# Gather of the token rows one pair ahead, kept totals inside the last gate-up product, last down weights in column halves, and the down biases in the third expert pair

## What is computed

```python
def expert_step(acc, xs):
    wgu, bgu, wdn, bdn, c = xs
    gu = jnp.matmul(hx, wgu) + bgu
    gate = jnp.minimum(gu[:, 0::2], SWIGLU_LIMIT)
    up = jnp.clip(gu[:, 1::2], -SWIGLU_LIMIT, SWIGLU_LIMIT)
    act = gate * jax.nn.sigmoid(SWIGLU_ALPHA * gate) * (up + 1.0)
    y = jnp.matmul(act, wdn) + bdn
    return acc + c[:, None] * y.astype(jnp.float32), None
...
hx = layer_norm(DN_ALPHA * hx + f, ln2_g, ln2_b)
```

## Time and profile before

| what | before |
|---|---|
| time, median of 3 runs (lowest to highest) | 1141.97 us (1140.39 to 1142.9) |
| time of the profiled execution | 1139.37 us |
| its span, first to last instruction | 1137.5 us |
| TensorE matmul busy | 1099.5 us (97%) |
| VectorE busy | 293.1 us (26%) |
| ScalarE busy | 203.6 us (18%) |
| mean DMA rate over the span | 399 GB/s |

### The profile page before, as it was taken

The page is one execution under the profiler, slowest core; times in us unless marked ns, Lnnn a source line. Parts: engine busy times, 40 slices in busy tenths (PEclk is TensorE's granted clock), DMA queues, the critical chain, the costliest instruction groups (busy, mean ns, idle before and its releaser), DMA issues.

```text
span 1137.5 us, 14116 instructions
## 1 busy us (share of the span) xinstructions
PE 1099.5 (97%) x5468; PEld 463.2 (41%) x5469; DVE 293.1 (26%) x734; ACT 203.6 (18%) x481; POOL 30.0 (3%) x65
## 2 busy tenths in 40 slices
PE   8999999999999999999999999999999999999996
PEld 6876764433333333333333333333333333333331
DVE  1553757530303030212121212120203031303033
ACT  2323412411111120202020202020201111111102
POOL 0110111000000000000000000000000000000001
PEclk9999999999999999999999999999999999999998
DMA  9967878999999999999999999999999999999994
GB/s 361 351 219 248 285 280 336 426 433 407 430 421 430 430 431 430 431 430 429 432 431 432 432 430 432 432 432 429 433 430 432 432 430 432 431 430 430 425 426 160
DMA packets 59172, 454.37 MB, mean 399 GB/s; under 512 B 6467, under 2 KB 19411, under 8 KB 31348
## 3 DMA queue, kind: packets, MB, share of 16 engines
q1 hardware_dynamic: 56642, 440.97, 92.7%
q0 software_dynamic: 1728, 10.75, 2.5%
q10 hardware_dynamic: 754, 1.98, 0.4%
HBM read 450.14 MB, written 11.93 MB: 406 GB/s over the span
## 4 chain that ended last, share of the span: by engine, by line
PE 83%; DMA 13%; ACT 2%; DVE 2%; issue 1%; SPq 0%; DVEq 0%
PE bank L1171 30%; PE bank L1224 19%; DMA ring<-in_w_gate_up 13%; PE bank L732 6%; PE bank L759 6%; PE bank L1055 5%; PE bank L1251 3%; PE bank L762 2%; PE bank L920 2%; PE bank L1051 1%; PE bank L1354 1%; PE bank L1267 1%; PE bank L877 1%; ACT ybuf L1417 1%; ACT actT L1417 1%; PE bank L851 1%
## 5 line engine op out<-in xcount | busy, mean ns | idle before, releaser
L1171 PE MATMUL bank<-ring,xg 128*64 128x512 f32 x2032 | 445.6, 594 | 10.8 <-DMA ring<-in_w_gate_up 10.8
L1171 PEld LDWEIGHTS bank<-ring,xg 128*64 128x64 f32 x2032 | 146.4, 137 | 299.3 <-issue 296.9
L1224 PE MATMUL bank<-ring,actT 128*64 128x512 f32 x960 | 216.2, 597 | 4.2 <-ACT actT L1417 4.2
L2080 DVE TENSOR_TENSOR acc<-acc,bank 128x512 f32<-128x512 f32 x60 | 41.3, 688 | 492.0 <-PE bank L1251 491.8
L1571 ACT ACTIVATE sig<-gate 128x256 f32<-128x256 f32 x64 | 26.5, 416 | 530.1 <-DVE gate L2062 530.1
L1224 PEld LDWEIGHTS bank<-ring,actT 128*64 128x64 f32 x960 | 67.3, 137 | 120.0 <-issue 115.3
L2062 DVE TENSOR_SCALAR gate<-bank 128x256 f32<-128x256 f32 x64 | 26.8, 419 | 186.8 <-PE bank L1171 186.8
L759 PE MATMUL bank<-xT,wblk 128*128 128x288 f32 x256 | 65.4, 409 | 0.3 <-DVE xT L1670 0.3
L1562 ACT ACTIVATE xg<-bank,small 128x128 f32<-128x128 f32 x128 | 48.0, 457 | 97.0 <-PE bank L732 96.9
L1055 PE MATMUL bank<-hx,pick 128*128 128x512 f32 x128 | 59.2, 605 | 0.0
L1417 ACT ACTIVATE ybuf<-bank 128x512 f32<-128x512 f32 x63 | 36.0, 596 | 126.7 <-PE bank L1224 87.4
(11 more groups left out here) (247 smaller groups left out, 672.3 us busy)
## 6 DMA issues: line engine op xcount, KB each, us to landing
ring<-in_w_gate_up SPq DMA_DIRECT2D x127, 2048.0 KB, 26.5
ring<-in_w_down SPq DMA_DIRECT2D x63, 2048.0 KB, 28.0
wblk<-in_w_in SPq DMA_DIRECT2D x11, 1024.0 KB, 8.7
kring<-in_cache_k_moba SPq DMA_DIRECT2D x16, 256.0 KB, 7.5
vring<-in_cache_v_moba SPq DMA_DIRECT2D x16, 256.0 KB, 7.2
out<-in_state_k_win POOLq DMA_DIRECT2D x8, 512.0 KB, 5.2
out<-in_state_v_win POOLq DMA_DIRECT2D x8, 512.0 KB, 6.1
kring<-in_state_k_win SPq DMA_DIRECT2D x16, 256.0 KB, 5.3
```

Of the source, the lines that this page charges most:

```text
L1171: ins = nc.tensor.matmul(bank[n][64 * e:64 * e + 64, :], xg[:, k, 64 * e:64 * e + 64], w[e][:, 512 * n:512 * n + 512], start=False, stop=( ...
L1224: ins = nc.tensor.matmul(bank[4 + half][64 * e:64 * e + 64, :], actT[:, j, 64 * e:64 * e + 64], w[e][:, at:at + 512], start=(j == 0), stop ...
L2080: V.tensor_tensor(o, o, new, ALU.add).then_inc(S.added, 1)
```

## The change

It does five things. `gather(i + 2)` stands behind k = 5 of `gate_up(i + 1)`, and only `gather(1)` still stands behind `gate_up(0)`; ACT takes the gathered rows at the end of `between_pairs`. In the last pair `combine` moves to k = 1, the first three `keep_sums` into `gate_up` behind k = 4 (`keep_first`, in banks 4, 5 and 7), and both activation halves are turned in bank 6. The last row chunk of `w_down` is loaded in two column halves, and ACT copies both halves of the last result, the lower one when its own matmuls are done. The products of the down biases go from pair 12 to pair 2. Some loads share a semaphore: the attention table now counts on `blk_in` and `ln_g` on `bdn_in`, and DVE waits for the second LayerNorm's parameters later.

```diff
+    Y_BANK, SUM_BANK = (0, 1), ((4, 5), (2, 3), (7,))
...
-    MIDDLE = 12
+    MIDDLE = 2
...
-            for c in range(2):
-                sp.dma_start(dst[:, :, c, :], src[:, :, 2 + c, :]).then_inc(half_in[8 + c], 16)
+            sp.dma_start(dst[:, :, 0, :], src[:, :, 2, :]).then_inc(half_in[8], 16)
+            for half in range(2):
+                h = slice(512 * half, 512 * half + 512)
+                sp.dma_start(dst[:, :, 1, h], src[:, :, 3, h]).then_inc((S.lower_in, half_in[9])[half], 16)
...
         def finish(i, m, odd, m_next, whole=True, next_whole=True):

-            gather(i + 1, i * 2)
+            if isinstance(i, int) and i == 0:
+                gather(1, 0)
             turn_weights(i, i * 2 + 3)
             turn_act(i, i * 2 + 4)
             down(i, m, odd, {0: lambda: turn_slots(i + 1, 0),
                              1: lambda: (pe.wait_ge(S.actT_ready, i * 2 + 2), turn_slots(i + 1, 1))}, whole)
             if m_next is not None:
-                gate_up(i + 1, m_next, (odd + 1) % PERIOD, {3: lambda: combine(i)}, next_whole)
+                gate_up(i + 1, m_next, (odd + 1) % PERIOD, {3: lambda: combine(i), 5: lambda: gather(i + 2, i * 2 + 2)}, next_whole)
...
-            gather(i + 1, i * 2)
             turn_weights(i, i * 2 + 3)
             turn_act(i, i * 2 + 4)
             down(i, m, odd, {0: first_slots, 1: other_slots, 2: other_biases}, True)
             pe.wait_ge(S.bias_added, 5)
-            gate_up(i + 1, m_next, (odd + 1) % PERIOD, {3: lambda: combine(i)}, True)
+            gate_up(i + 1, m_next, (odd + 1) % PERIOD, {3: lambda: combine(i), 5: lambda: gather(i + 2, i * 2 + 2)}, True)
...
-        finish(2, 0, 2, 1)
+        finish_with_biases(MIDDLE, 0, 2, 1)

         def finish_three(m):
             finish(m * PERIOD, m, 0, m)
             finish(m * PERIOD + 1, m, 1, m)
             finish(m * PERIOD + 2, m, 2, m + 1)

-        with pe.Fori(1, MIDDLE // PERIOD) as m:
+        with pe.Fori(1, PAIRS // PERIOD - 1) as m:
             finish_three(m)
-        finish_with_biases(MIDDLE, MIDDLE // PERIOD, 0, MIDDLE // PERIOD)
-        finish(MIDDLE + 1, MIDDLE // PERIOD, 1, MIDDLE // PERIOD)
-        last = PAIRS - 1
-        finish(last - 1, last // PERIOD - 1, 2, None)
+        last, final = PAIRS - 1, PAIRS // PERIOD - 1
+        finish(last - 3, final, 0, final)
+        finish(last - 2, final, 1, final)
+        finish(last - 1, final, 2, None)

         def keep_sums(t, half, stop=False):

             if t == 2:
-                return nc.tensor.matmul(bank[7][:, 0:256], ident, acc_s[:, :], start=True, stop=stop)
-            return nc.tensor.matmul(bank[2 * t + half][:, :], ident, acc[:, t, 512 * half:512 * half + 512],
+                return nc.tensor.matmul(bank[SUM_BANK[2][0]][:, 0:256], ident, acc_s[:, :], start=True, stop=stop)
+            return nc.tensor.matmul(bank[SUM_BANK[t][half]][:, :], ident, acc[:, t, 512 * half:512 * half + 512],
                                     start=True, stop=stop)

-        def last_down():
-
-            turn_act(last, 2 * last + 2, (0,))
+        def keep_first():
             pe.wait_ge(S.added, 5 * last + 5)
             keep_sums(0, 0)
             keep_sums(0, 1)
-            pe.wait_ge(S.actT_ready, last * 2 + 1)
             keep_sums(2, 0)
+
+        def turn_last(a):
+            pe.wait_ge(S.act_ready, last * 4 + 2 * a + 2)
+            pe.wait_ge(*((S.actT_ready, 2 * last + 1) if a else (S.spread_ready, last + 1)))
+            for j in range(4 * a, 4 * a + 4):
+                f = 512 * a
+                ins = turn(bank[6][:, 128 * (j % 4):128 * (j % 4) + 128], up[:, f + j % 4:f + 512:4])
+            ins.then_inc(S.act_turned, 1)
+
+        def last_down():
+
+            turn_last(0)
             for v in range(4):
                 w = ring[slot_of(0, 8 + v)]
                 if v < 3:
...
                 pe.wait_ge(S.actT_ready, last * 2 + (1 if v < 2 else 2))
                 for c in range(2):
                     j = 2 * v + c
-                    if v == 3:
-                        pe.wait_ge(half_in[8 + c], 16)
+                    if j == 6:
+                        pe.wait_ge(half_in[8], 16)
                     for half in range(2):
+                        if j == 7:
+                            pe.wait_ge((S.lower_in, half_in[9])[half], 16)
                         for e in range(2):
                             at = 2048 * e + 1024 * c + 512 * half
-                            ins = nc.tensor.matmul(bank[4 + half][64 * e:64 * e + 64, :], actT[:, j, 64 * e:64 * e + 64],
+                            ins = nc.tensor.matmul(bank[Y_BANK[half]][64 * e:64 * e + 64, :], actT[:, j, 64 * e:64 * e + 64],
                                                    w[:, at:at + 512], start=(j == 0), stop=(j == KC - 1))
+                        if j == 7 and half == 0:
+                            ins.then_inc(S.lower_done, 1)
                 if v < 3:
                     ins.then_inc(S.unit_used, 1)
                 if v == 0:
-                    turn_act(last, 2 * last + 2, (1,))
+                    turn_last(1)
                     keep_sums(1, 0)
                 if v == 1:
                     keep_sums(1, 1)

         def mix_last():

-            pe.wait_ge(S.y_ready, last * 2 + 2)
             for j in (0, 1, 4, 2, 3):
                 t, half = divmod(j, 2)
+                pe.wait_ge(S.y_ready, last * 2 + (1 if j == 0 else 2))
                 if t == 2:
-                    ins = mix_samples(bank[7], False)
+                    ins = mix_samples(bank[SUM_BANK[2][0]], False)
                 else:
-                    ins = nc.tensor.matmul(bank[j][:, :], spread[:, 128 * t:128 * t + 128],
+                    ins = nc.tensor.matmul(bank[SUM_BANK[t][half]][:, :], spread[:, 128 * t:128 * t + 128],
                                            ybuf[:, 512 * half:512 * half + 512], start=False, stop=True)
                 ins.then_inc(S.mixed, 1)

-        gate_up(last, last // PERIOD, 0, {3: lambda: combine(last - 1), 5: lambda: turn_weights(last, 2 * last + 1)})
+        gate_up(last, last // PERIOD, 0, {1: lambda: combine(last - 1), 4: keep_first, 5: lambda: turn_weights(last, 2 * last + 1)})
...
-        def take_turned(i, halves=(0, 1)):
+        def take_turned(i, halves=(0, 1), banks=(7, 6)):
             for a in halves:
                 act.wait_ge(S.act_turned, i * 2 + (a + 1))
-                copy(actT[:, 4 * a:4 * a + 4, :], bank[7 - a][:, :].rearrange("p (k s) -> p k s", k=4)).then_inc(
+                copy(actT[:, 4 * a:4 * a + 4, :], bank[banks[a]][:, :].rearrange("p (k s) -> p k s", k=4)).then_inc(
...
         sigmoids(0)
-
-        def between_pairs(i):
-            take_gathered(i + 1)
+        take_gathered(1)
+
+        def between_pairs(i, gathers=True):
             take_weights(i)
             take_turned(i)
             take_slots(i + 1)
             take_down(i)
+            if gathers:
+                take_gathered(i + 2)

         def between_with_biases(i):
-            take_gathered(i + 1)
...
-        between_pairs(PAIRS - 2)
+        between_pairs(PAIRS - 2, False)
         sigmoids(PAIRS - 1, (0, 1))
         take_weights(PAIRS - 1)
-        take_turned(PAIRS - 1, (0,))
+        take_turned(PAIRS - 1, (0,), (6, 6))
         sigmoids(PAIRS - 1, (2, 3))
-        take_turned(PAIRS - 1, (1,))
+        take_turned(PAIRS - 1, (1,), (6, 6))
...
-        def take_lower():
-            act.wait_ge(S.down_done, PAIRS)
-            copy(ybuf[:, 0:512], bank[4][:, :]).then_inc(S.y_ready, 1)
+        def take_halves():
+            for half in range(2):
+                act.wait_ge(*((S.down_done, PAIRS) if half else (S.lower_done, 1)))
+                copy(ybuf[:, 512 * half:512 * half + 512], bank[Y_BANK[half]][:, :]).then_inc(S.y_ready, 1)

         nc.scalar.activation(s_(c_junk), s_(c_junk), ACT.Sqrt)
-        further_passes(act, more, none, first=take_lower, otherwise=take_lower)
+        further_passes(act, more, none, first=take_halves, otherwise=take_halves)
...
-        def take_upper():
-            dve.wait_ge(S.down_done, PAIRS)
-            V.tensor_copy(ybuf[:, 512:1024], bank[5][:, :]).then_inc(S.y_ready, 1)
-
         def sums_to_sbuf():
-            take_upper()
             for n, j in enumerate((0, 1, 4, 2, 3)):
...
-        dve.wait_ge(S.ln2_in, 160)
...
+        dve.wait_ge(S.ln2_in, 160)
```

More of the change, by code:

```diff
@@ L545, in _ @@
         sp.dma_start(hx[64 + E:65 + E, 2, :], ln1_b[0:1, :]).then_inc(S.bdn_in, 16)
-        sp.dma_start(ln_g[:, :], ln1_g[0:1, :].broadcast_to([128, D])).then_inc(S.ln1_in, 16)
+        sp.dma_start(ln_g[:, :], ln1_g[0:1, :].broadcast_to([128, D])).then_inc(S.bdn_in, 16)
         sp.wait_ge(S.msq_done, 8)
@@ L774, in mean_squares @@
             if n == 0:
-                pe.wait_ge(S.blk_in, 32)
+                pe.wait_ge(S.blk_in, 48)
             if n < 4:
@@ L1649, in _ @@
         for half in range(2):
```

(15 more changed lines are left out.)

16 lines of the change are left out of this document (8 added, 8 removed).

## The result

The change is slower: 1169.38 us median (1166.81 to 1171.1) against 1142.2 for the kernel before, ratio 1.0239 with an interval of 1.0216 to 1.0261. The forecast was 1154.3, slower by 1.1%. The page of the changed kernel first: span, TensorE's busy share, the granted clock and GB/s in 40 slices, and the transposes of the activation with the idle time before them.

The account below looks back on a forecast made before the run. It took TensorE's time per pair as the bound, at 57.5 us. Last gate-up end +14.2, down product -1.3 and first copy -0.6 make +12.3 us on 1141.97: 1154.3 us, 1.1% slower, range 1147 to 1161.

Parts of the forecast that it names:

- What bounds the kernel: Middle pairs: TensorE needs 55.74 us, the weight stream 58.35; at the end both are within 2 us, TensorE's pair time decides.
- G(14): G(i) is the end of pair i's gate-up product; G(14) was forecast at 1059.5 us for the change.
- G(15) = 1099.4: Last gate-up product's end if only the stream held it, 1.7 us sooner than in the kernel before.
- hidden after all: Rival: pair growth under 0.57 us, gather and totals hidden in DMA waits, time falls 3.6 to 1138.4 us; chance 0.04.
- The early gather: Each middle pair: gather adds 4.7 us inside gate-up, down product starts 2.9 sooner; +1.8, 57.5 us a pair.
- The clock: Two idle spells of about 1 us close together in each pair; TensorE's granted clock expected to stay at 1.00.
- clock rival: TensorE at 1.2 GHz in 16 matmuls behind the spells, 3.65 us doubled, 14 times: +51, about 1205 us; chance 0.02.
- Pair by pair: Summing the stretches from pair 0 on: last gate-up product ends at 1115.3 us, 14.2 later than before.
- The biases: Down-bias products moved from pair 12 to pair 2: their 5.0 us cost fully if TensorE bounds throughout.
- The last rows: Kernel's end: down product 1.3 us sooner, taking 19.1; first copy 0.6 sooner, leaving 15.3; column halves bring nothing.
- The fuller ring: TensorE's lag behind the stream grows to about 23 us; the stream idles more, but the lag is not used up.

Follow-up runs that it names:

- late_gather: The change with every gather behind the gate-up product again and ACT taking the gathered rows there: 1143.06 us, ratio 1.0011 to the kernel before.
- filled: The change with a useless identity matmul in each of the two idle spells before the activation's transposes: 1158.44 us, ratio 1.0150 to the kernel before.
- gather_only: The kernel before with only the early gather and ACT's taking of gathered rows from the change: 1167.03 us, ratio 1.0232.
- filled_first: The change with a useless matmul only in the first idle spell, ahead of the activation's first half: 1158.08 us, ratio 1.0145 to the kernel before.
- filled_second: The change with a useless matmul only in the second idle spell, between the activation's halves: 1157.22 us, ratio 1.0139 to the kernel before.

## Why the prediction was wrong

The direction and the mechanism it named first were right, the range was not. By its steps:

- **What bounds the kernel**: right up to G(14), but for a count: the stretch from G(7) to G(8) is held by the stream too, so five stretches have its waits and not four. Its figure for the end, G(15) = 1099.4 by the stream, was of no use, since from G(14) = 1044.6 on the stream no longer holds TensorE. The "hidden after all" rival at 1138.4 was priced with it, and `late_gather`, which is close to that case, came out at 1143.06.
- **The early gather, +1.8 us a pair**: right in kind. The two waits are where they were forecast, at 1.1 and 1.0 us. The sum was mis-sized: a pair takes 57.8, so +2.1, shown without the clock by `filled`. Half of the missing 0.3 is the down product's start: 6.9 us behind G in most pairs before and 4.14 now, so 2.76 are won and not 2.9. The other half is the gather, which costs 4.85 inside the gate-up product and not 4.7. Thirteen pairs make 3.9 us of it.
- **The clock**: this is the step that failed. The forecast read a clock of 1.00 from windows with single waits of 1.21 and 0.96 us, more than 19 us apart, and carried that over to two spells with 0.75 us between them. It gave the clock rival 0.02. In the profile the clock fell in 7 of 14 pairs, each time for 3.4 or 6.8 us, and cost 13.3 us, the excess of these stretches over those of `filled`, 57.8 (62.8 for pair 2 with the biases, 58.2 for the one behind it). By the medians it is 10.9 us; the profiled execution, 1171.1 us, is the longest of the change's four. The rival's price was too high, since the dips come in half of the pairs and cost 1.3 to 2.9 each and not 3.65; its chance was far too low. The Trainium skill, "TensorE: Matmul & The Clock Gate", part 1, has the rule that an idle TensorE has this clock lowered; the trace agrees in kind, since between G(0) and the last matmul the clock falls only at pairs with two idle spells, and filling either takes the dips away. That spells of 1.1 us are enough is what these runs show.
- **Pair by pair**: the forecast's G(15) = 1115.3 became 1135.1. Of these 19.8 us the clock is 13.3, the size of a pair 3.9, the stretch behind the biases 0.4, first and last stretch 0.45. Another 1.75 are the first stage, which ends at G(0) = 247.9 in this profile and between 246.2 and 248.9 in the profiles of the other kernels; that is scatter between executions and not the change.
- **The biases**: their 5 us are paid early in full, as forecast for a kernel that TensorE bounds (62.8 against 57.8 in `filled`, and 0.4 more in the stretch behind).
- **The last rows**: 19.13 against 19.1 and 15.0 against 15.3. Column halves without effect, as forecast: they landed 21 us before they were read. The forecast took the last unit's second half to be read 3.5 us before the last down matmul ends; that is its first half, and the second is read 1.8 before the end, which changes nothing here.
- **The fuller ring**: right that it does not run dry. The rate falls to 403 and 404 GB/s in the second and third stretch, but no wait of TensorE for a unit appears.

Without the clock the forecast would have stood: `filled`, which differs from the change only in two useless matmuls a pair and the wait ahead of each, is 4.1 us above 1154.3 and inside the range.

## What to carry to other kernels

Work that stands between a product and the use of its activation is cover: before moving it, sum up what DVE and ACT need behind the last matmul, since that much idle time comes back at the same place. Where two waits of a microsecond come close together, reckon with TensorE's clock and not with the waits alone; if the cover can't be had, a matmul that serves nothing in the wait can be cheaper than the dip (here 10.9 us cheaper). And when a stream holds a loop at some points, work that moves past the first of these points delays the loop's end even though waits remain behind it.

## What was not expected of the hardware

- Two idle spells of 1.1 us with 0.75 us of transposes between them brought the clock to its lower level in 7 of 14 pairs in the change's profile and in 3 of 14 in that of `gather_only`, one such spell in none of 14 (`filled_first` and `filled_second`). In the kernel before each middle pair has waits of 0.3 to 0.4 and 0.2 to 0.3 us there and no dip.
- The dip outlasts the spells and can begin behind them: in pair 1 the clock is still 1.00 at 312 us, when matmuls run again, and at 0.50 from 313.1 to 316.5; in pair 7 it falls inside the second spell, at 668.1, and stays down for 6.8 us. A busy TensorE in the row says nothing of it: the 16 records of 5.35 us count as 5.35 us of work.
- A matmul that does nothing useful, added 14 times in one place, made the kernel some 12 us faster (1169.38 to 1157.22; the ratios to the kernel before, 1.0239 and 1.0139, give 11.4).
